# Rotary pairs moved by GpSimd's transfers, and scores as two split products on stacked parts

## The reference

```python
def _partial_rotary(x, pos):
    half = ROT_DIM // 2                      # 8
    ...
    x1 = x[..., :half].astype(jnp.float32)
    x2 = x[..., half:ROT_DIM].astype(jnp.float32)
    rot = jnp.concatenate([x1 * cos - x2 * sin, x2 * cos + x1 * sin], axis=-1).astype(x.dtype)
    return jnp.concatenate([rot, x[..., ROT_DIM:]], axis=-1)

def _sliding_window_sink_attention(q, k, v, sinks):
    ...
    s_meta = jnp.einsum("bnqkgd,bmkd->bkgnqm", qb, km).astype(jnp.float32) * scale
    s_band = jnp.einsum("bnqkgd,bnjkd->bkgnqj", qb, k_band).astype(jnp.float32) * scale
    ...
    probs = jax.nn.softmax(jnp.concatenate([s_meta, s_band, sink_col], axis=-1), axis=-1)
```

## Time and profile before

| | |
|---|---|
| median of three runs | 3173.88 us (3172.31 to 3174.22) |
| profiled execution | 3176.35 us, span 3174.8 us, TensorE clock granted 0.995 |
| TensorE busy | 3119.4 us (98%) |
| VectorE busy | 2196.6 us (69%) |
| ScalarE busy | 1557.9 us (49%) |
| GpSimd busy | 335.7 us (11%) |

### The profile page before, as it was taken

The page is one execution under the profiler, slowest core; times in us unless marked ns, Lnnn a source line. Parts: engine busy times, 40 slices in busy tenths (PEclk is TensorE's granted clock), DMA queues, the critical chain, the costliest instruction groups (busy, mean ns, idle before and its releaser), DMA issues.

```text
span 3174.8 us, 59919 instructions
## 1 busy us (share of the span) xinstructions
PE 3119.4 (98%) x23211; PEld 2925.7 (92%) x23211; DVE 2196.6 (69%) x2897; ACT 1557.9 (49%) x2538; POOL 335.7 (11%) x343
## 2 busy tenths in 40 slices
PE   8999999999999999999989999999999999999998
PEld 7899999999999998898889999999998888888898
DVE  7678888888888888876675655656457566556535
ACT  5355555555555555442263645556226455555521
POOL 1000000000000000000001342250000124314000
PEclk9999999999999999999999999999999999999999
DMA  6334444433434435452344222223324322221522
GB/s 209 92 97 107 111 111 113 127 106 106 112 103 108 117 95 191 116 171 88 106 133 120 69 69 78 81 75 111 109 94 146 107 81 80 75 81 60 174 95 92
DMA packets 461728, 342.81 MB, mean 108 GB/s; under 512 B 20504, under 2 KB 451544, under 8 KB 458352
## 3 DMA queue, kind: packets, MB, share of 16 engines
q1 hardware_dynamic: 443712, 296.28, 32.3%
q0 software_dynamic: 8304, 26.92, 2.4%
q10 hardware_dynamic: 9552, 17.37, 1.6%
HBM read 315.04 MB, written 25.46 MB: 107 GB/s over the span
## 4 chain that ended last, share of the span: by engine, by line
PE 80%; DVE 8%; DVEq 4%; DMA 3%; ACT 3%; issue 2%; SPq 0%; ACTq 0%
PE ps L777 13%; PE ps L778 13%; PE ps L779 13%; PE ps L949 7%; PE ps L951 7%; PE ps L952 7%; DVE w_low_blocks L2230 2%; DMA w_raw_blocks<-in_w_in 2%; PE ps L1204 2%; PE ps L1368 1%; PE ps L1364 1%; PE ps L1366 1%; PE ps L784 1%; PE ps L1019 1%; PE ps L785 1%
## 5 line engine op out<-in xcount | busy, mean ns | idle before, releaser
L777 PE MATMUL ps<-x_high,w_high_layer 128*128 128x264 f32 (+3 forms) x2560 | 801.6, 313 | 13.3 <-DVE x_low L2624 10.9
L779 PE MATMUL ps<-x_high,w_low_layer 128*128 128x264 f32 (+3 forms) x2560 | 769.2, 300 | 0.0
L778 PE MATMUL ps<-x_low,w_high_layer 128*128 128x264 f32 (+3 forms) x2560 | 768.3, 300 | 0.0
L777 PEld LDWEIGHTS ps<-x_high,w_high_layer 128*128 128x128 f32 x2560 | 482.7, 189 | 33.9 <-issue 16.9
L949 PE MATMUL ps<-x_high_rows,w_high_blocks 128*128 128x256 f32 x1815 | 507.4, 282 | 2.7 <-DVE v_gelu_feature_major L2263 1.3
L778 PEld LDWEIGHTS ps<-x_low,w_high_layer 128*128 128x128 f32 x2560 | 484.1, 189 | 19.1 <-issue 3.3
L951 PE MATMUL ps<-x_low_rows,w_high_blocks 128*128 128x256 f32 x1792 | 498.8, 278 | 0.0
L779 PEld LDWEIGHTS ps<-x_high,w_low_layer 128*128 128x128 f32 x2560 | 482.5, 188 | 16.8
L952 PE MATMUL ps<-x_high_rows,w_low_blocks 128*128 128x256 f32 x1792 | 497.5, 278 | 0.0
L1486 ACT ACTIVATE w_high_blocks<-w_raw_blocks 128x1024 fp32r<-128x1024 f32 x280 | 295.9, 1060 | 267.1 <-PE ps L952 186.4
L2140 DVE TENSOR_TENSOR w_low_layer<-w_raw,w_high_layer 128x1024 fp32r<-128x1024 f32 x212 | 261.8, 1240 | 224.4 <-ACT w_high_layer L1407 222.4
(11 more groups left out here) (533 smaller groups left out, 6076.6 us busy)
## 6 DMA issues: line engine op xcount, KB each, us to landing
w_raw_blocks<-in_w_in SPq DMA_DIRECT2D x200, 512.0 KB, 5.1
w_raw<-in_w_in SPq DMA_DIRECT2D x384, 256.0 KB, 3.2
w_raw<-in_w_out SPq DMA_DIRECT2D x224, 256.0 KB, 3.0
w_raw_blocks<-in_w_out SPq DMA_DIRECT2D x24, 512.0 KB, 5.6
residual<-residual_stream ACTq DMA_DIRECT2D x8, 1056.0 KB, 9.3
residual_stream<-y_layer ACTq DMA_DIRECT2D x2, 2176.0 KB, 11.4
x_natural<-in_x SPq DMA_DIRECT2D x4, 1024.0 KB, 9.4
x_feature_major<-x_stage POOLq DMA_DIRECT2D x4, 1024.0 KB, 7.9
```

Source lines behind the costliest of these rows:

```text
L777: pe.matmul(dst, hi[j][:, kt, wc], x_hi[:, r, tok], start=first, stop=False)
L778: pe.matmul(dst, hi[j][:, kt, wc], x_lo[:, r, tok], start=False, stop=False)
L779: return pe.matmul(dst, lo[j][:, kt, wc], x_hi[:, r, tok], start=False, stop=last)
```

## The change

No matrix rotates any more. GpSimd copies the pairs: for q of each group, each half t as soon as ScalarE has copied it, four transfers of 8 partitions x 528 (or 512) put each row on its partner's place in `swap`; for k of each layer four transfers of 8 x 2 x 528. The sign lies in the table of sines. `swap` shares its memory with `q_odd_heads`.

VectorE multiplies `swap` with the sines and writes the rotated q to `roped[t]` (`tmp`, `c_partial`). ScalarE then rounds each head's 64 rows to their high part (`queries`), on 64 partitions of `qst[h]`; VectorE writes the low part on the other 64 partitions of the same tile. The keys are stacked too: `k_high_low` holds the key's high part twice, and in a second block its low part twice. A score is then two fp32r products, q's stack by the high block and by the low block. `stack_high` and `stack_low` count them. VectorE and GpSimd have their groups written out instead of a loop, and TensorE's waits in front of the rotations move to the first score or fall away.

```diff
         vm = nc.alloc_sbuf_tensor_at("v_meta_pair", [P, P], F32, offset=hole + NM * 4)
-        rot = nc.alloc_sbuf_tensor_at("rotation", [P, P], F32, offset=hole + (NM + P) * 4)
-        kz = rr.take("k_zero_padded", [P, 2, 3, NM + 2 * BLK])
+        ks = rr.take("k_high_low", [P, 2, 3, NM + 2 * BLK], F32R)
         vz = rr.take("v_group", [P, ST, HD])
...
         ma0 = rw.take("first_mask", [P, NM + BLK])
+        q_odd = rw.take("q_odd_heads", [P, 2, L], F32R)
+        swap = q_odd[:].bitcast(F32)
+        qst = (nc.alloc_sbuf_tensor_at("q_even_heads", [P, 2, L], F32R, offset=big), q_odd)
+        assert rw.at <= limit
...
         rgs = t1
+        roped = (t1, cacc)
...
                 pool.wait_ge(x_ready, (5 + 3 * l) * KT)
-                pool.dma_start(rot[:], consts[:, K_ROT:K_MASK0]).then_inc(shape_in, 16)
                 pool.dma_start(ma0[:], consts[:, K_MASK0:K_MASK]).then_inc(shape_in, 16)
                 pool.dma_start(kshape[:], consts[:, K_MASK:K_ALL]).then_inc(shape_in, 16)
                 pool.dma_start(small[:, 0:NH], a["attn_sinks_2"][ds(l, 1)].squeeze(0).partition_broadcast(P)).then_inc(sink_in, 16)
-                with pool.Fori(0, NKV) as g:
+                pool.wait_ge(zeros_ok, l + 1)
+                pool.wait_ge(evac, 2 * (U_LAYER + N_LAYER * l + O_K2) + 2)
+                for o in (0, PAIR, HD, HD + PAIR):
+                    d = o ^ PAIR
+                    pool.dma_start(swap[d:d + PAIR, :, :], krw[o:o + PAIR, :, :]).then_inc(pairs_swapped[0], 16)
+                for g in range(NKV):
...
                                            w[:, ds(8 * l + 2 * g + o, 1), :]).then_inc(rw_in, 16)
+                    for t in range(2):
+                        pool.wait_ge(evac, 2 * (U_LAYER + N_LAYER * l + O_GRP + 4 * g) + t + 1)
+                        for o in (0, PAIR, HD, HD + PAIR):
+                            d = o ^ PAIR
+                            pool.dma_start(swap[d:d + PAIR, t, cc], qrw[o:o + PAIR, t, cc]).then_inc(pairs_swapped[t], 16)
...
-                def rotate_k():
-
-                    pe.wait_ge(evac, 2 * (U + O_K2) + 2)
-                    pe.wait_ge(shape_in, 48 * (l + 1))
-                    pe.wait_ge(pl_ok, l + 1)
-                    for t in range(2):
-                        for q in range(2):
-                            last = pe.matmul(ps[:, 4 + 2 * t + q, 0:LH], rot[:], krw[:, t, q * LH:(q + 1) * LH], start=True, stop=True)
-                        last.then_inc(rotk_mm, 1)
-
-                unit(U + O_GRP, fill, wide=True, hook=lambda n: rotate_k() if n == 1 else None, real=(real, real))
+                unit(U + O_GRP, fill, wide=True, real=(real, real))
...
-                    def rotate(t):
-
-                        if t == 0:
-                            pe.wait_ge(evac, 2 * V + 2)
-                            pe.wait_ge(k_roped, 2 * (l + 1))
+                    def score(i, n):
+                        q = qst[i % 2][:, i // 2, :]
+                        bank = 4 + n % 2
+                        if n == 0 and i % 2 == 0:
+                            pe.wait_ge(stack_low, 3 * G + i // 2 + 2)
+                        if n == 0 and i == 0:
+                            pe.wait_ge(pl_ok, l + 1)
                             pe.wait_ge(r_act, 2 * G)
-                            pe.wait_ge(o_taken, 2 * G)
                             if not real:
                                 pe.wait_ge(mo_ready, 2 * G)
-                        for q, c in enumerate(parts):
-                            last = pe.matmul(ps[:, 4 + 2 * t + q, 0:c.stop - c.start], rot[:], qrw[:, t, c], start=True, stop=True)
-                        last.then_inc(rot_mm, 1)
-
-                    def score(i, n):
-                        q = qrw[:, i // 2, :]
-                        bank = 4 + n % 2
-                        if n == 0 and i == 0:
-                            pe.wait_ge(rope_done, 2 * G + 2)
-                            pe.wait_ge(kz_ready, G + 1)
                         pe.wait_ge(s_taken, 4 * A + 4 * i + n + 1)
                         tq = NM + n * BLK
                         w = NM + (2 if n else 1) * BLK
-                        last = pe.matmul(ps[:, bank, 0:w], q[:, tq:tq + BLK], kz[:, i % 2, max(n - 1, 0), 0:w],
-                                         start=True, stop=True)
+                        for m in range(2):
+                            last = pe.matmul(ps[:, bank, 0:w], q[:, tq:tq + BLK], ks[:, m, max(n - 1, 0), 0:w],
+                                             start=(m == 0), stop=(m == 1))
                         if n == 0 and not real:
-                            last = pe.matmul(ps[:, bank, 160:160 + NM], q[:, 0:BLK], kz[:, i % 2, 0, 0:NM],
-                                             start=True, stop=True)
+                            for m in range(2):
+                                last = pe.matmul(ps[:, bank, 160:160 + NM], q[:, 0:BLK], ks[:, m, 0, 0:NM],
+                                                 start=(m == 0), stop=(m == 1))
                         last.then_inc(s_done, 1)
...
                             n += first
-                            if n == 8:
-                                rotate(0)
-                                rotate(1)
-                            elif n >= 11:
+                            if n >= 11:
                                 step(n - 11)
...
                         k = krw[s * HD:(s + 1) * HD, ds(gp, 1), :].squeeze(1)
-                        z = kz[h * HD:(h + 1) * HD, h]
+                        z = ks[h * HD:(h + 1) * HD, 0]
                         for e in range(3):
...
+                    def queries(t):
+
+                        act.wait_ge(rope_done, 2 * G + t + 1)
+                        for h in range(2):
+                            o = h * HD
+                            last = act.activation(qst[h][o:o + HD, t, cc], roped[t][o:o + HD, cc], ACT.Copy)
+                        last.then_inc(stack_high, 1)
+
                     act.wait_ge(s_done, 4 * A)
...
                     keys(0)
-                    keys(1).then_inc(kz_ready, 1)
+                    keys(1).then_inc(stack_high, 1)
                     high(V + 1, 2)
                     take(V, 1, cols(qrw[:, 1, :]), banks(2))
                     high(V + 1, 3)
+                    queries(0)
+                    queries(1)
                     act.wait_ge(c_taken, G)
...
                 dve.memset(cra[:, 0:TAPS - 1], 0.0)
-                dve.memset(kz[HD:P, 0], 0.0)
-                dve.memset(kz[0:HD, 1], 0.0)
                 dve.memset(vm[:], 0.0)
+                dve.memset(swap[:], 0.0)
                 dve.memset(rx[:, 0:RTAPS - 1], 0.0).then_inc(zeros_ok, 1)
...
                 dve.tensor_scalar(q, z, 8.0, None, ALU.mult)
-                dve.wait_ge(shape_in, 48 * (l + 1))
+                dve.wait_ge(shape_in, 32 * (l + 1))
+                dve.wait_ge(pairs_swapped[0], 64 * (NKV * l + l + 1))
                 dve.wait_ge(sink_in, 16 * (l + 1))
...
                     dve.drain()
-                    dve.wait_ge(rotk_mm, 2 * l + m + 1)
-                    dve.tensor_tensor(two(t1[:]), halves(4 + 2 * m), two(sin), ALU.mult)
+                    dve.tensor_tensor(t1[:], swap[:, m, :], sin, ALU.mult)
                     dve.tensor_tensor(k, k, cos, ALU.mult)
                     dve.drain()
                     dve.tensor_tensor(k, k, t1[:], ALU.add).then_inc(k_roped, 1)
-                with dve.Fori(0, NKV) as g:
+                for g in range(NKV):
                     V = U + O_GRP + 4 * g
...
-                        q = qrw[:, t, :]
+                        q, r = qrw[:, t, :], roped[t]
                         dve.drain()
-                        dve.wait_ge(rot_mm, 2 * G + t + 1)
-                        dve.tensor_tensor(cols(t1[:]), banks(4 + 2 * t), cols(sin), ALU.mult)
+                        dve.wait_ge(pairs_swapped[t], 64 * (G + 1 + (l + 1 if t == 0 else 0)))
+                        dve.tensor_tensor(r[:, cc], swap[:, t, cc], sin[:, cc], ALU.mult)
                         dve.tensor_tensor(q[:, cc], q[:, cc], cos[:, cc], ALU.mult)
                         dve.drain()
-                        dve.tensor_tensor(q[:, cc], q[:, cc], t1[:, cc], ALU.add).then_inc(rope_done, 1)
-
-                    lows(V + 1)
+                        dve.tensor_tensor(r[:, cc], q[:, cc], r[:, cc], ALU.add).then_inc(rope_done, 1)
+
+                    def queries(t):
+
+                        dve.wait_ge(stack_high, 3 * G + t + 2)
+                        for h in range(2):
+                            o, d = h * HD, (1 - h) * HD
+                            last = dve.tensor_tensor(qst[h][d:d + HD, t, cc], roped[t][o:o + HD, cc],
+                                                     f(qst[h][o:o + HD, t, cc]), ALU.subtract)
+                        last.then_inc(stack_low, 1)
+
+                    def keys():
+
+                        dve.wait_ge(stack_high, 3 * G + 1)
```

(20 more changed lines are left out.)

17 lines of the change are left out of this document (8 added, 9 removed).

## The result

The changed kernel takes 3139.97 us (median of 4 runs, 3136.23 to 3143.51), the kernel before took 3174.05 beside it (4 runs, 3172.31 to 3174.34). The ratio is 0.9897, interval [0.9884, 0.9909] (the quotient of the two medians, 0.9893, lies inside it). It is faster by 34 us, 3 short of the forecast of 3137 and inside its range. The profiled execution is the slowest of the four, 3143.51 us with a span of 3142.0.

A forecast was written before the change was run, and what follows sets the result against it. TensorE, busy 98% of the span, was taken to bound the kernel. Terms 20.2 + 19.6 - 2.7 - 0.4 = 36.7 us, off the median of 3173.88, gave 3137 us, range 3131 to 3152.

The forecast's parts named there:

- Rotations: Rotating q and k leaves TensorE in eight groups, with waits for q's copy in layer 1: 19.6 us saved.
- Scores: On TensorE, 96 long f32 scores become two split products each, 0.25 instead of 0.46 us: 20.2 us saved.
- the transpose: A group's first transpose on TensorE waits for GpSimd's normalised block after shorter scores: 0.05 x 8 = 0.4 us lost.
- Fourth low weight: VectorE delivers it late to TensorE, 0.3 us in three layer 0 groups, 0.6 in three of layer 1: 2.7 lost.
- Short scores: The 32 scores of 144 columns on TensorE gain 0, since each pass has a floor near 0.12 us.
- (d): Short scores gain by their columns, 3.5 us, and the low weights are not late: 3131 us, chance 0.09.
- The swaps: GpSimd's transfers of swapped q and k pairs land in 2.0 us, in time for VectorE: cost 0.
- The prediction's own sign of being wrong: On VectorE, a rotation's first multiplication released by a DMA, or the third low weight being waited for.
- (b): Swapped pairs landing after 8.4 us cost 5.7 us in eight groups: slower, 3179 us; decides from about 7.5; chance 0.05.
- (a): Swaps landing after 4.4 us, or small subtractions costing 0.25 each: TensorE waits, 3146 us, 3152 with both; chance 0.20.
- (c): Split score pairs on TensorE miss the projection's pitch, 0.40 us instead of 0.25, gain 14 less: 3152 us, chance 0.05.
- (e): TensorE waits as long for VectorE as it saves, needing 5 us a group: 3174 us, chance 0.03.

The follow-up runs named there:

- transfers only: Kernel before with q and k pairs swapped by GpSimd transfers, f32 scores kept, all four low weights ahead of both rotations: 3151.24 us, ratio 0.9939.
- the loops: Kernel before with only the group loops of VectorE and GpSimd written out: 3170.84 us beside 3171.21, ratio 0.9998.
- the earlier low weight: Changed kernel with the fourth low weight moved ahead of low keys and queries on VectorE: 3128.73 us, ratio 0.9867; repeated, 3133.64 us.
- The nine memsets: Changed kernel with nine small GpSimd memsets between the copy of q's first half and its four transfers: 3175.30 us, ratio 1.0007.
- The twenty: Changed kernel with twenty small GpSimd memsets between the copy of q's first half and its four transfers: 3186.48 us, ratio 1.0043.
- the scores alone: Split scores in the changed kernel's order, but rotation kept on TensorE as in the kernel before: 3174.35 us, ratio 1.0009.
- two orders: Split scores with rotation kept on TensorE, fourth low weight behind low keys and queries (3174.35 us) or ahead of them (3151.95 us).

## Why the prediction was right, and where it was off

**Step by step, in the stretches.** Forecast, then measured:

- Rotations 19.6: 19.7 (transfers only, less the loops).
- Loops 0: 1.1, from one profile of each kernel.
- Scores 20.2, less 0.4 for the transpose: 18.7, the difference between transfers only and the earlier low weight (855.7 - 837.0), no late low weight in either. Place by place: 88 of the 96 long scores give 0.20 each, 17.7 together; the eight in front of the transpose that waits for ScalarE give nothing in sum, a loss of 1.6 where 0.4 was booked; the short ones give 0.7, and 0.3 lies elsewhere.
- Fourth low weight 2.7: 4.6 (841.65, the mean of the two profiles, less 837.1). The mechanism was right in each detail: six groups, the first group of each layer free, layer 1 twice layer 0. By the difference of the groups it is 0.3 to 0.6 us in layer 0 and 0.8 to 1.1 in layer 1, instead of 0.3 and 0.6. The term was undersized because keys and queries take 0.35 longer than reckoned from wider operations, which is 2.1 in six groups, against the 1.9 missing.

19.7 + 1.1 + 18.7 - 4.6 = 34.9. That this is the measured sum is no evidence by itself: the four are differences along a row of kernels that starts and ends with the two compared. What counts is that each was measured apart and came near its forecast. Two terms fell short of the forecast, by 1.1 and 1.9, and the loops gave 1.1 that was not booked. The median lay 3 us from 3137 the first time and on it the second (3137.4); medians repeat no better than that, so the last microseconds of agreement are luck.

**Short scores, booked at 0.** Nearly right: over all 32 places the gain is 0.7 us (0.02 in 16 of them, with the 16-column companion of layer 0 or without it, nothing in eight, 0.05 in eight), and widening the short scores cost 1.2. Rival (d), 3.5 us from columns, is wrong.

**The swaps, booked at 0.** Right for q's first half, which decides over the low weights, with 1.1 us of slack where 0.9 was reckoned. For the second half the landing was wrong and the price right: it was to land 3.8 us after its copy with 2.3 to spare, landed 4.8 to 6.3 after it in six groups, and left 0.7 to 1.4 us in five of them and nothing in the sixth. For k the step failed: the pairs were to land 3.8 us after the copy, landed 8.5 and 9.2 after it, and VectorE stood 2.6 and 3.4 us waiting for them. It was saved by room behind it that the prediction had not looked for. The prediction's own sign of being wrong, a first multiplication of a rotation released by a DMA, thus showed for k and cost nothing.

**Rival (b), slower by a late landing.** Its price holds in size. By its working pairs that come 6.4 us later cost 5.7 a group, and every microsecond less takes one off. The nine memsets made them 5.2 later on average, which is 4.5 x 8 = 36; the stretches grew by 39. The twenty made them 7.3 later, 6.6 x 8 = 53; they grew by 51. It decides from 5.5 us more than usual by the prediction, and at 5.2 the gain is gone (1.0007). In kind it was incomplete: only two thirds of the 39 are TensorE's waits, the rest is the clock behind them, which was priced nowhere. And a delay of 3.6 us was enough, since the weight stream made 5 to 6 of it.

**Rivals (a), (c), (e).** None shows in the time. Landings as late as (a) supposed are there, for k and for some of q's second halves (up to 4.5), but not for the first halves, the only ones that (a)'s price hangs on. Split pairs keep the projection's pitch, against (c).

**The two parts were added up, and they don't add in any order.** Rotation and scores gave 19.7 and 18.7 in the changed kernel, but the scores alone, in the same order of VectorE's queue, gave -5.8. That went unnoticed in the prediction, since it priced only the sum.

## What to carry to other kernels

Put what the bounding engine needs soonest first in the helper's queue, and let work with slack stand behind it: of two orders with the same instructions one was 25 us faster. Price a wait of the bounding engine with what follows it, and a delay of a transfer with what it will then travel beside. When time outside the changed code moves by more than the effect, compare stretches between marks that both kernels have.

## What the hardware did that was not expected

- A wait of TensorE of about 2 us was followed, in five groups of eight, by 12 to 16 products at 1.2 GHz; in the kernel with twenty memsets, where the waits were 3.8 to 4.5, in all eight, by 14 to 24. None followed the waits of up to 0.83. What decides between 2 us with and without was not settled; it isn't the length alone, since by distance of starts a wait of 1.94 had such a stretch behind it and one of 2.27 had none.
- Time outside the changed stretches differed by 9 us (2291.0 to 2300.2) over fourteen profiles of the same code, nearly all of it before the first stretch begins (1674.2 to 1683.1); its cause was not looked for.
- Swaps of one size landed after 1.8 us with the DMA engines 12% busy and after up to 4.5 with them 49% to 60% busy, and the memsets that moved the first halves into the weight stream (73%) made these late and most of the second halves punctual. So for these it is what a transfer travels beside, and not its size, that makes it late. Whether the 33 KB of k's swaps add to their 4.8, at 72% to 79%, stays open.
